# Neighbourhood attention bias of a column band: one addition over four heads, and queries that carry the scale

## The reference, cut to what matters

```
scale = HEAD_DIM ** -0.5                       # 1/8
s_nb  = einsum(q, k_gathered) * scale + bias   # bias: rpb by (dr, dc), -inf outside the 16 columns
s_ctx = einsum(q, k_context) * scale           # no bias
p     = softmax(concatenate([s_nb, s_ctx]))
o     = p_nb @ v_gathered + p_ctx @ v_context
```

## Time and profile before

| what | value |
|---|---|
| median of three runs | 1955.42 us (1955.2 to 1959.95) |
| the profiled execution's own time | 1959.76 us |
| its span | 1957.9 us |
| TensorE, VectorE, ScalarE, GpSimd busy | 89%, 50%, 31%, 7% |
| mean granted TensorE clock | 0.94 of full |
| na attention, layer 0 and layer 1 | 44 us and 36 us of the span |

### The profile page before, as it was taken

How to read it: one execution, slowest core, us unless ns; L and a number is a source line. 1 busy time by engine, 2 the same in 40 slices (tenths; PEclk the granted TensorE clock), 3 DMA queues, 4 the chain that set the end, 5 groups by cost and what they waited for, 6 DMA issues and landing times.

```text
span 1957.9 us, 24632 instructions
## 1 busy us (share of the span) xinstructions
PE 1734.9 (89%) x10460; PEld 1530.1 (78%) x10460; DVE 983.6 (50%) x1606; ACT 598.9 (31%) x798; POOL 146.5 (7%) x184
## 2 busy tenths in 40 slices
PE   2699988858979999999999979998747899999996
PEld 1699955656959999999999959985546577887874
DVE  7844437783785554554632372125684443233334
ACT  3222224742242222221122142234443333232231
POOL 1000000000500000000000410001000300000003
PEclk9799998858989999999999989999868999999998
DMA  8343341000414434333322222234100223332332
GB/s 317 137 129 122 126 67 51 1 2 33 130 35 138 129 104 144 112 126 118 129 65 65 76 83 65 74 96 60 40 2 22 65 76 97 97 97 86 97 97 97
DMA packets 80238, 176.61 MB, mean 90 GB/s; under 512 B 38896, under 2 KB 39408, under 8 KB 79872
## 3 DMA queue, kind: packets, MB, share of 16 engines
q1 hardware_dynamic: 67008, 123.62, 21.0%
q0 software_dynamic: 13120, 51.41, 7.5%
HBM read 172.91 MB, written 2.10 MB: 89 GB/s over the span
## 4 chain that ended last, share of the span: by engine, by line
PE 80%; DVE 13%; ACT 2%; DMA 2%; issue 2%; DVEq 0%; SPq 0%; ACTq 0%
PE psum L700 69%; PE psum L806 2%; PE psum L817 2%; PE psum L762 2%; DMA ada_0a<-in_adaT 1%; DVE f_t L1109 1%; PE psum L840 1%; DVE s_sb L1155 1%; DVE hk L1277 1%; DVE x L1113 1%; DVE hd L1291 1%; PE psum L730 1%; DVE tmp L1087 1%; DVE psum L1353 1%; DVE hq L1284 1%
## 5 line engine op out<-in xcount | busy, mean ns | idle before, releaser
L700 PE MATMUL psum<-h_hi,w_hi 128*128 128x384 f32 (+1 forms) x1872 | 550.6, 353 | 44.6 <-DVE h_lo L1094 28.2
L700 PE MATMUL psum<-h_lo,w_hi 128*128 128x384 f32 (+1 forms) x1872 | 548.3, 352 | 0.0
L700 PE MATMUL psum<-h_hi,w_lo 128*128 128x384 f32 (+1 forms) x1872 | 547.7, 352 | 0.0
L1016 DVE TENSOR_TENSOR w_lo<-raw,w_hi 128x1024 fp32r<-128x1024 f32 x194 | 239.9, 1237 | 469.0 <-ACT w_hi L498 469.0
L700 PEld LDWEIGHTS psum<-h_hi,w_hi 128*128 128x128 f32 x1872 | 346.4, 191 | 69.0 <-issue 44.9
L498 ACT ACTIVATE w_hi<-raw 128x1024 fp32r<-128x1024 f32 x194 | 205.8, 1061 | 564.2 <-DMA raw<-in_wstream 564.1
L700 PEld LDWEIGHTS psum<-h_lo,w_hi 128*128 128x128 f32 x1872 | 347.0, 191 | 19.6
L700 PEld LDWEIGHTS psum<-h_hi,w_lo 128*128 128x128 f32 x1872 | 346.3, 190 | 19.9
L1027 DVE CUSTOM_DVE_ANT_0 psum<-ada_w,c_b 128x1024 f32<-128x1024 f32 x160 | 206.3, 1289 | 8.5 <-DVE ada_t L1027 0.2
L1055 DVE TENSOR_TENSOR tmp<-tmp,psum 128x768 f32<-128x768 f32 (+1 forms) x44 | 36.1, 821 | 282.1 <-PE psum L700 282.1
L700 PE MATMUL psum<-hid_hi,w_hi 128*128 128x384 f32 (+1 forms) x528 | 160.8, 359 | 15.3 <-DVE w_lo L1016 13.2
(11 more groups left out here) (167 smaller groups left out, 1473.0 us busy)
## 6 DMA issues: line engine op xcount, KB each, us to landing
raw<-in_wstream SPq DMA_DIRECT2D x196, 512.0 KB, 3.5
ada_w<-in_adaT POOLq DMA_DIRECT2D x80, 512.0 KB, 4.1
ada_0a<-in_adaT SPq DMA_DIRECT2D x6, 1024.0 KB, 14.1
fn_l<-in_dftL POOLq DMA_DIRECT2D x2, 2048.0 KB, 8.0
na_r<-in_rpb SPq DMA_DIRECT2D x64, 64.0 KB, 3.7
x<-in_xT POOLq DMA_DIRECT2D x2, 1536.0 KB, 14.3
ada_0b<-in_adaT SPq DMA_DIRECT2D x2, 1024.0 KB, 19.0
out_xT<-x SPq DMA_DIRECT2D x4, 512.0 KB, 2.8
```

The lines of the kernel that those rows point to most:

```text
L700: mm = pe.matmul(ps[u][:, at:at + hi - lo], w[:, slot, k], r[:, k, lo:hi], start=first, stop=last)
L1016: dve.tensor_tensor(w_lo[:, k % RING].rearrange("p c n -> p (c n)"), raw[:, k % RING], w_hi[:, k % RING].rearrange("p c n -> p (c n)").bit ...
```

## The change

Three things are changed. The staged queries `na_q` are multiplied by SCALE when GpSimd stages them: the copy becomes a tensor_scalar with a multiplication by 1/8. The scores of the four bands (local and context keys) so come out scaled; the context tiles of layer 0, whose queries are not staged, keep the old way. The bias then needs no factor, and the four instructions per band on VectorE become one tensor_tensor addition over all four heads, 1024 elements per partition. The negated maximum and the exponential use a scale of 1 for the scaled tiles and 1/8 for the others.

```diff
+        def score_scale(kind, tile):
+            return 1.0 if kind == "na" and tile[0] else SCALE
...
                     for r in range(2):
                         q = u_t[:, QA + r, 0:LAT].rearrange("p (r c) -> p r c", c=GRID_W)
-                        ins = pool.tensor_copy(na_q[:, cb % 2, r].rearrange("p (r c) -> p r c", c=16),
-                                               backwards(q[:, :, 16 * cb:16 * cb + 16]))
+                        ins = pool.tensor_scalar(na_q[:, cb % 2, r].rearrange("p (r c) -> p r c", c=16),
+                                                 backwards(q[:, :, 16 * cb:16 * cb + 16]), SCALE, None, ALU.mult)
                     ins.then_inc(na_st, 1)
...
-                            act.activation(p, p, ACT.Exp, bias=nb[:, s % 3, j:j + 1], scale=SCALE,
+                            act.activation(p, p, ACT.Exp, bias=nb[:, s % 3, j:j + 1],
+                                           scale=score_scale(kind, tiles[s // 2]),
                                            accum_out=sums[:, s % 3, j:j + 1]).then_inc(at_p, 1)
...
-                    for h in range(4):
-                        v = na_b[:, 4 * (cb % 2) + h].rearrange("p (r c) -> p r c", c=BAND)
-                        m = na_m[:, cb].unsqueeze(1).to_broadcast([P, ROWS, BAND])
-                        r = na_r[:, cb % 2].rearrange("p (r h c) -> p r h c", r=ROWS, h=4)[:, :, h]
-                        ins = dve.scalar_tensor_tensor(v, r, 1.0 / SCALE, m, ALU.mult, ALU.add)
-                    ins.then_inc(na_bias, 1)
+                    v = na_b[:, 4 * (cb % 2):4 * (cb % 2) + 4].rearrange("p h (r c) -> p h r c", c=BAND)
+                    m = na_m[:, cb].unsqueeze(1).unsqueeze(1).to_broadcast([P, 4, ROWS, BAND])
+                    r = na_r[:, cb % 2].rearrange("p (r h c) -> p h r c", r=ROWS, h=4)
+                    dve.tensor_tensor(v, r, m, ALU.add).then_inc(na_bias, 1)
                     dve.wait_ge(na_bias, 4 * l + cb + 1)
...
                     if kind == "na":
-                        dve.tensor_scalar(nb[:, s % 3], mx[:, s % 2], -SCALE, None, ALU.mult).then_inc(at_n, 1)
+                        dve.tensor_scalar(nb[:, s % 3], mx[:, s % 2], -score_scale(kind, tiles[s // 2]), None, ALU.mult)\
+                           .then_inc(at_n, 1)
```

## The result

| | kernel before | changed kernel |
|---|---|---|
| median, 20 runs each on one chip | 1957.23 us | 1962.29 us |
| lowest to highest | 1954.76 to 1960.15 | 1957.17 to 1965.12 |
| the profiled execution and its span | 1959.76 and 1957.9 | 1963.05 and 1961.3 |

The ratio is 1.0023, interval [1.0016, 1.0031]: slower by 4.5 us (3 to 6). The forecast was 1962.1 us, so the total came out almost as predicted. The reason given for it did not: the term that was to make up all of it is zero in the trace, and others that had been set small take its place.

What follows compares the result with a forecast made beforehand. TensorE was taken to bound the kernel (busy 89%, 80% of the chain). Layer 0 +7.1 us (+7.5 - 0.42) and layer 1 -0.3, about +6.7, on the median 1955.42 gave 1962.1 us; range 1954.8 to 1968.0.

Steps and rivals of the forecast that it cites:

- What the forecast held likeliest: Whole kernel: slower by over 0.3%, chance 0.63; a load on the path of 6.3 to 10 us had 0.58.
- The GpSimd code load: Before layer 0's band 0 queries: GpSimd's first arithmetic loads code for 7.1 us, so TensorE starts 7.5 us later.
- The test that the forecast set itself: Layer 0: a tensor_scalar starting within 0.3 us of the copies means the main step is wrong and Rival (a) holds.
- Rival (a): Layer 0 staging: no code load on the path; sum -0.4 us, 1955.0 us, unmeasurable; chance 0.14.
- Staging: Band 0's queries: two tensor_scalar at 0.49 us replace copies; pair 0.4 us later, +0.35 in layer 0, +0.1 in layer 1.
- The forecast's second sign: GpSimd staging: a tensor_scalar over 1 us for 128 elements means staging was mis-sized, and layer 1 shows it alone.
- Rival (e): Shared GpSimd/VectorE port: the long addition blocks band 1's staging, 1.2 us at most against 5 us slack; no own chance.
- The clock: TensorE's clock at layer 0's first scores after the 7 us gap: charged 0, ends -1.5 to +1.5 us.
- rival (d): Layer 0: the gap slows TensorE's clock, 1.5 us more, 1963.6 us; no own chance, included in the 0.58 case.
- Bias addition: VectorE, four bands on the chain: one 1.22 us addition replaces 1.43 us, saving 0.21 each, 0.84 us in all.
- the 0.27 us of band 0 in layer 1: Layer 1, band 0: at most 0.27 us from an earlier bias end, taken back by the staging.

Runs made afterwards that it cites:

- merge_only: Changed kernel with the merged addition kept, queries copied on GpSimd as before, scale moved into ScalarE's copy out of the projection: 1957.73 us, ratio 1.0007.
- before_again: The kernel before, unchanged, run and profiled once more: ratio 1.0001.
- late_layer1: Kernel before plus four superfluous GpSimd value copies ahead of band 0's queries in layer 1 alone: 1962.1 us, ratio 1.0029.
- the fills: 12 idle transposes ahead of both layers' HGRN output products, in the kernel before, merge_only and after_warm: ratios 0.9984, 0.9983, 0.9990.
- after_warm: Changed kernel plus 12 idle TensorE transposes ahead of the wait for band 0's queries: 1961.15 us, ratio 1.0021.
- late_copies: Kernel before plus four superfluous GpSimd value copies ahead of band 0's queries in both layers: 1966.43 us, ratio 1.0046.
- before_fill: Kernel before plus 12 idle TensorE transposes in the wait ahead of the HGRN output products, both layers: 1954.41 us, ratio 0.9984.

## Why the prediction was right in its total and wrong in its reason

**The total.** The forecast put a step of 6.7 us on a median of three executions, 1955.42 us. Twenty give 1957.23, and the step is 4.5 us (5.1 by the medians). A base 1.8 us low and a step about 2 us high nearly cancel, and the step came from a term that measures nothing: 1962.1 against 1962.29 is luck. What the forecast held likeliest, a loss of over 0.3%, did not come either; the loss is 0.23%.

**The GpSimd code load** (7.1 us, "This term decides"). This is the step that failed. The records moved to where it said, but cost nothing: 2.05 us with them in layer 0, 2.06 without them in layer 1, 1.04 with them once VectorE keeps away, 2.06 with them moved to the head of the program. The two records of 13 ns were the lower end of the term, and the lower end was right. The reading "records of a load, hence a fetch, hence the price of a cold DMA" had three steps, and only the first stood in a row. The test that the forecast set itself, a start within 0.3 us of the copies, came out against it: 0.10 us. Rival (a), for which that test was to speak, holds in its mechanism and fails in its time: 1955.0 was the sum without the load, and it left out what follows. The Trainium skill's figure of about 6 us ("GPSIMD Engine Reference", section 2.1) is not borne out by any run here either.

**Staging** (pair +0.4 us, +0.35 and +0.1 on the path). Mis-sized. The single tensor_scalar was well placed: 0.53 measured, 0.49 taken. The pair of band 0 took 2.05 instead of 0.53, +1.5 us, in both layers: 0.5 for the scaling itself (an undisturbed pair takes 1.03) and 1.0 for the addition beside it. The forecast's second sign, over 1 us for 128 elements, so came with the second tensor_scalar, and in both layers. What was missed is that the merge makes of four instructions of 0.42 us, between which GpSimd gets through, one of 1.22 us, and that it starts while GpSimd stages the very queries that TensorE needs. The price was in the earlier trace rows: the four took 2.06 instead of 1.43 us beside GpSimd. It was read as a cost to VectorE alone.

**Rival (e), the shared port.** Its mechanism was the right one, set at the wrong band. It was written off since band 1 has 5 us of slack; merge_only shows just that, at band 1, free of charge. With the slower tensor_scalar the addition reaches band 0's second query instead, where GpSimd had 0.05 us of slack. The Trainium skill, "SBUF — State Buffer", section "Who interferes with whom", has VectorE instructions on two SBUF inputs contend with GpSimd's own reads. The runs agree: 1.53 and 1.55 us for a tensor_scalar that began just behind such an addition, 0.53 for the others.

**The clock** (0, ends ±1.5; rival (d) +1.5). The right rival with too low a price and too short a reach. It was weighed only at the first scores of layer 0, for a gap of 7 us. It struck in layer 1, at a gap of 2.30 us, and went further than those 16 matmuls: 0.38 us there, 1.0 in the bands behind, and 1.3 to 3.7 us in the HGRN stage (72.9 and 75.3 against 71.6). Over all 14 profiles the first scores of layer 1 took 3.0 to 3.6 us in the five where TensorE had waited 2.30 us or more, and 2.00 us in the nine where it had waited 1.50 us or less. In layer 0 the picture is not clean: they took 3.3 to 3.8 us in the four with 2.30 us or more, but also 3.4 to 3.7 in three of the ten with less (before, before_again and late_layer1, at 0.88 us). late_layer1 shows by intervention that a delay alone brings the slow scores of layer 1 and a loss of more than the delay. That the clock, and not the delay, is most of the change's cost is shown for two profiles by their stages: 1.35 us of the 5.8 and 3.1 us are direct. For the medians it is not shown: the fills point that way within their noise, and after_warm alone speaks against a simple form of it.

**Bias addition** (0.21 us per band, four bands, 0.84). The instruction was right to 4 ns (1218 measured, 1.22 expected, eight of them). The gain was halved: in both layers the distance from band 2 to band 3 fell from 7.21 to 7.11, 0.10 instead of 0.21 us. VectorE was taken to work without a gap; but the odd unit's score addition, which followed f_t's copy after 0.34 us (304.77 to 305.11), now follows after 0.43 (303.57 to 304.00). That it comes up against TensorE's scores there is the likely reason, not tested. Of the 0.27 us of band 0 in layer 1 nothing came: the first score addition stood 1.30 us behind the start of TensorE's scores in the kernel before (1345.49 to 1346.79) and as much in after_warm (1345.30 to 1346.60), so the bias was not what held it.

**Sum by the measured terms**, layer 1: +1.45 for the queries, +1.38 for the clock inside the stage and -0.10 for the addition make +2.73 us; the stages behind add 0.4 to 3.1 (layer 1's sum less 2.7). Layer 0: the same 1.43 us of delay, and no change in the sum of its stages. The kernel before had the low clock at layer 0's first scores already, so there was less to lose; that this is the reason was argued and not tested, and late_copies, whose layer 0 sum is 2.1 us above late_layer1's (259.7) for a delay of 2.0 us, lost something there with the same low clock at its first scores.

**Left open.** What sets the clock back in one execution of a program and not in another; why after_warm's profile and its median disagree; why merge_only's HGRN ran at the low clock without a late attention. These are of the size of the effect, and 12 runs with one trace each do not settle them.

## What to carry to other kernels

Before an instruction of one engine is merged into a longer one, look at what the engine that shares its memory port is doing at that moment and who waits for that: here a microsecond that nobody needed on VectorE was taken from GpSimd, on which all waited, and holding the addition back by one wait gave most of the loss back. Time in which TensorE stands still can cost more than itself (2.0 us cost 3.3 to 8.2 us in late_layer1), and the profiles show part of it as a lower clock in stages that the change does not touch; compare by stage, with the granted clock beside it, and try a few idle matmuls in the gap. And a record whose meaning is guessed gets both ends of its price in the forecast, not the one of the nearest large number.

## What the runs showed of the hardware that was not expected

- The MODIFY_POOL_CONFIG records ahead of GpSimd's first tensor_scalar cost nothing that can be seen: with the addition held back, layer 0's pair took 1.04 us with them and layer 1's 1.03 without.
- A GpSimd tensor_scalar of 128 fp32 elements took 0.53 us, a copy of the same 0.295. It took 1.55 when it began 0.05 us behind the start of a VectorE addition of 1.22 us on two SBUF operands, and the addition lost nothing. Where the addition began while GpSimd was copying (merge_only), the copies already begun kept their time, the addition took 1.46 us, and the first copy begun behind it 1.39 instead of 0.40.
- Four superfluous copies of 1.82 us in front of one wait cost 5.7 us (late_layer1), and 1.5 us of idle transposes in another gap, once a layer, gained 3 us (before_fill).
